# The delta branch's output norm in two halves, other places for its pieces, and other queues for some loads

## The reference, cut to what matters

```python
def merge(att, dn, z):
    gated = rms_norm(dn, dn_norm_g) * silu(z)        # per head of 64
    cat = concatenate([att, gated], axis=-1)         # 512 + 512 wide
    return cat @ w_out
dn_sum_c, dn_sum_l = bidir_delta(dn_c, dn_l, with_ctx_out)   # chunks of 64 tokens, both directions
out_l = merge(att_l, dn_sum_l, dz_l)                 # latents
out_c = merge(att_c, dn_sum_c, dz_c)                 # context tokens
```

## Time and profile before

| | us |
|---|---|
| median of 3 runs (1579.77 to 1584.63) | 1582.9 |
| the profiled execution | 1587.52 |
| its span | 1585.4 |
| PE busy in it | 1436.4 (91%) |
| DVE busy in it | 890.6 (56%) |
| ACT busy in it | 589.3 (37%) |
| POOL busy in it | 113.3 (7%) |
| mean TensorE clock, as a share of full speed | 0.951 |

### The profile page before, as it was taken

The page is one execution under the profiler, slowest core; times in us unless marked ns, Lnnn a source line. Parts: engine busy times, 40 slices in busy tenths (PEclk is TensorE's granted clock), DMA queues, the critical chain, the costliest instruction groups (busy, mean ns, idle before and its releaser), DMA issues. The chain is left out here.

```text
span 1585.4 us, 30140 instructions
## 1 busy us (share of the span) xinstructions
PE 1436.4 (91%) x13235; PEld 1180.1 (74%) x13235; DVE 890.6 (56%) x1279; ACT 589.3 (37%) x937; POOL 113.3 (7%) x113
## 2 busy tenths in 40 slices
PE   4798998899998698998999999899999998899998
PEld 2566676787887377766777888678888677799998
DVE  3548543544454547345446322769785764688854
ACT  3224535121212224233324211544463553455534
POOL 0000000233232000000000000000001430000000
PEclk7899989799999798999999999899999998899999
DMA  9221110244225121555554222223243003466652
GB/s 320 83 80 53 54 38 16 68 136 158 87 60 158 53 80 53 159 160 159 159 160 133 90 97 86 67 80 105 82 133 107 1 1 117 123 172 181 183 184 107
DMA packets 170764, 172.24 MB, mean 109 GB/s; under 512 B 15270, under 2 KB 135946, under 8 KB 170634
## 3 DMA queue, kind: packets, MB, share of 16 engines
q1 hardware_dynamic: 169328, 169.33, 35.1%
q10 hardware_dynamic: 1306, 0.99, 0.2%
HBM read 169.26 MB, written 1.05 MB: 107 GB/s over the span
## 5 line engine op out<-in xcount | busy, mean ns | idle before, releaser
L306 DVE TENSOR_TENSOR w_lo<-w_raw,w_hi 128x2048 fp32r<-128x2048 f32 (+1 forms) x99 | 225.3, 2276 | 289.6 <-ACT w_hi L296 289.4
L619 PE MATMUL bank<-h,w_hi 128*128 128x512 f32 (+2 forms) x1032 | 361.6, 350 | 26.6 <-issue 14.4
L622 PE MATMUL bank<-h,w_hi 128*128 128x512 f32 (+2 forms) x1032 | 352.0, 341 | 0.0
L623 PE MATMUL bank<-h,w_lo 128*128 128x512 f32 (+2 forms) x1032 | 351.8, 341 | 0.0
L296 ACT ACTIVATE w_hi<-w_raw 128x2048 fp32r<-128x2048 f32 (+1 forms) x99 | 187.9, 1898 | 292.4 <-PE bank L619 189.5
L619 PEld LDWEIGHTS bank<-h,w_hi 128*128 128x128 f32 (+1 forms) x1032 | 198.8, 193 | 65.9 <-issue 45.4
L622 PEld LDWEIGHTS bank<-h,w_hi 128*128 128x128 f32 (+1 forms) x1032 | 198.9, 193 | 23.3 <-issue 2.9
L623 PEld LDWEIGHTS bank<-h,w_lo 128*128 128x128 f32 (+1 forms) x1032 | 198.5, 192 | 22.2
L637 DVE SCALAR_TENSOR_TENSOR acc<-bank,params,acc 128x510 f32<-128x510 f32 (+3 forms) x272 | 172.1, 645 | 71.1 <-ACT acc L1372 46.0
L1372 ACT ACTIVATE acc<-bank,params 128x512 f32<-128x512 f32 (+1 forms) x88 | 47.7, 580 | 131.1 <-DVE ffn_g_lo L1389 49.8
L619 PE MATMUL bank<-h_hi,w_hi_hyb 128*128 128x512 f32 (+1 forms) x184 | 78.3, 425 | 12.7 <-DVE h_lo L594 4.9
(11 more groups left out here) (377 smaller groups left out, 2602.5 us busy)
## 6 DMA issues: line engine op xcount, KB each, us to landing
w_raw<-in_ffn_up SPq DMA_DIRECT2D x88, 512.0 KB, 5.3
w_raw<-in_mod_w SPq DMA_DIRECT2D x40, 1024.0 KB, 5.2
w_raw<-in_ffn_down SPq DMA_DIRECT2D x22, 1024.0 KB, 5.0
w_raw<-in_ssm_w_in SPq DMA_DIRECT2D x20, 1024.0 KB, 5.3
w_raw<-in_hyb_w_in SPq DMA_DIRECT2D x9, 1024.0 KB, 5.3
mod_early<-in_mod_w SPq DMA_DIRECT2D x8, 1024.0 KB, 11.0
w_raw<-in_ssm_w_out SPq DMA_DIRECT2D x8, 1024.0 KB, 4.8
w_raw<-in_hyb_w_in SPq DMA_DIRECT2D x8, 256.0 KB, 5.1
```

What stands on the lines that cost most here:

```text
L306: dve.tensor_tensor(lo, raw, hi.bitcast(F32), ALU.subtract).then_inc(k.lo_done.sem, 1)
L619: mm = pe.matmul(out, wh, xh, start=(start and n == 0), stop=False)
L622: pe.matmul(out, wh, xl, start=False, stop=False)
L623: mm = pe.matmul(out, wl, xh, start=False, stop=(stop and n == last))
```

## The change

The stage `stage_delta_out` is gone. Its work is done by a class `DeltaOut` that handles 256 tokens at a time, in pieces for each engine. The context tokens' pieces stand in the fourth pair and the tail of the solve. The latents' pieces stand in the first block of the product by the output matrix; for it, slot 0 takes both row blocks for one output tile after the other, with the sums after tile 1 and the spreads after tile 4. The split of the output matrix' first tile moves to the solve's tail. The last three modulation products move from the tail to the levels. In the start, the column groups 2 and 3 of `mod_w` are loaded by POOL's queue once the tokens have landed, the spread of the reciprocal root stands ahead of the third group's products, and the second tile's low part is made last on DVE. The solve's constants are loaded at the end of the attention block instead of at the start of the solve. Two more things move: the silu of z moves from the tail to the fourth pair, and the two weight buffers are numbered the other way round.

```diff
@@ stage_start
+            pool.wait_ge(k.s_in, 16 * (T // P))
+            for g in range(2, n_mod):
+                load_mod(pool, g)
...
-            issue_loads(k, sp, first + 2)
-            for g in range(2, n_mod):
-                load_mod(sp, g)
             issue_loads(k, sp, first + 4)
...
-            modulate(2)
             pe.wait_ge(recip_done.sem, recip_done.at(1))
...
+            modulate(2)
             modulate(3)
...
-            split_lo(k, dve, first + 1)
             mod_bias(k, dve, 0)
...
             low(KD - 1)
+            split_lo(k, dve, first + 1)
@@ stage_hyb_attention, SP
+            sp.wait_ge(mm_done.sem, mm_done.at(NC))
+            sp.dma_start(d.kc[:, :], a["k_dn"][:, 0:d.n_kc]).then_inc(s_k.sem, 16)
@@ RowGemm.pe
+            if self.out is not None and s == 2:
+                pe.wait_ge(self.out.l_done.sem, self.out.l_done.at(1))
+            if self.out is not None and s == 0:
+                for m in range(KD):
+                    if m == 6:
+                        pe.wait_ge(self.out.y_done.sem, self.out.y_done.at(2))
+                    split_matmuls(pe, self.bank(m)[:, 0:n], [pair(m, 0), pair(m, 1)], start=True, stop=False)
+                    if m == 1:
+                        self.out.pe_sums(pe)
+                    if m == 4:
+                        self.out.pe_spread(pe, 0)
+                        self.out.pe_spread(pe, 1)
@@ stage_delta_solve
-    for n, it in enumerate(sorted(list(range(13)) + [3, 6, 9]) + list(range(15, 20))):
+    for n, it in enumerate((0, 1, 2, 2, 3, 4, 5, 5, 6, 7, 8, 8, 9, 10, 11, 11, 14, 15, 16, 16, 17, 18, 18, 19)):
...
+                            if (lv, l) == (1, 0):
+                                o.pe_sums(pe)
+                            if (lv, l) == (2, 1):
+                                o.pe_spread(pe, 0)
+                            if (lv, l) == (3, 1):
+                                o.pe_spread(pe, 1)
             for n, (name, s) in enumerate(tail):
                 piece(name, s)
-                if n < 3:
-                    mod_products(k, pe, 29 + n)
-            mod_turn(k, pe, 2)
+                if n == 1:
+                    mod_turn(k, pe, 2)
@@ stage_delta_solve, ACT
+                        if lv == 0:
+                            act.activation(zT[:, :, :], zT[:, :, :], ACT.Silu).then_inc(zs_done.sem, 1)
+                            o.act_square(act)
+                        if lv == 1:
+                            o.act_root(act)
+                        if lv == 4:
+                            o.act_high(act)
...
                 if s == 6:
-                    act.activation(zT[:, :, :], zT[:, :, :], ACT.Silu)
+                    split_hi(k, act, first)
@@ stage_delta_solve, DVE
+                            if (lv, l) == (0, 0):
+                                dve.wait_ge(oc_done.sem, oc_done.at(4))
+                                o.dve_add(dve)
+                            if (lv, l) == (1, 1):
+                                o.dve_mean(dve)
+                            if (lv, l) == (2, 0):
+                                o.dve_recip(dve)
+                            if (lv, l) == (3, 0):
+                                o.dve_scale(dve, 0)
+                            if (lv, l) == (4, 0):
+                                o.dve_scale(dve, 1)
+                                dve.wait_ge(zs_done.sem, zs_done.at(1))
+                                o.dve_gate(dve)
             for name, s in tail:
                 piece(name, s)
+                if (name, s) == ("ks", 5):
+                    o.dve_low(dve)
+                if (name, s) == ("ds", 6):
+                    split_lo(k, dve, first)
@@ stage_layer0_tail, ACT and DVE
-            row0.act_splits(act, 1, 5)
+            out.act_square(act)
+            row0.act_splits(act, 1, 2)
+            out.act_root(act)
+            out.act_high(act)
+            row0.act_splits(act, 2, 5)
...
-            row0.dve_splits(dve, 1, 5)
+            out.dve_add(dve)
+            out.dve_mean(dve)
+            out.dve_recip(dve)
+            row0.dve_splits(dve, 1, 2)
+            out.dve_scale(dve, 0)
+            out.dve_scale(dve, 1)
+            out.dve_gate(dve)
+            out.dve_low(dve)
+            row0.dve_splits(dve, 2, 5)
```

158 lines of the change are left out of this document (81 added, 77 removed), and 4 rows, old and new, of the table TALLIES.

## The result

| | median us | runs | lowest to highest | profiled execution, span |
|---|---|---|---|---|
| before | 1583.96 | 15 | 1579.77 to 1589.46 | 1587.52, 1585.4 |
| changed | 1576.15 | 15 | 1570.45 to 1580.68 | 1573.66, 1571.9 |

The ratio is 0.9945 [0.9931, 0.9959]: 8.7 us faster. In seven more executions it was 0.9949 [0.9933, 0.9964]. The forecast was 17.1 us, and its range ended at 1574 us. The direction was right, half of the size is missing.

What follows compares the result with a forecast made beforehand. PE bounds the fourth pair, a dependent chain the tail, transfers the start. Terms -25.0 + 6.4 + 0.4 + 2.9 + 3.5 - 2.4 - 2.9 = -17.1 us took the median from 1582.9 to 1565.8, range 1556 to 1574.

Steps and rivals of the forecast that it cites:

- The stage, -25.0: Delta output stage, from the solve's end to the first product: goes entirely with one barrier, -25.0 us.
- the product, +3.5: Product by the output matrix: PE gains the latents' sums and spreads, 1.7 us each, the rest nearly hidden; +3.5 us.
- The start and the constants, -5.3 together: Program start -2.9 us, as a second queue fills transfer gaps; solve's constants loaded earlier, -2.4 us.
- their bound of 2.6: Solve's constants: the gain of 2.4 us was bounded between 0 and 2.6 us.
- The rival of POOL's late loads: Start: POOL's transfers begin only at 22 us, start gains 0, median 1568.7; chance 0.08, plus 0.02 for slower than before.
- PE and waits in the fourth pair: Solve's levels: added PE work of +6.4 us and waits of +0.4 us, the fourth pair taking 46 us instead of 40.8.
- +6.4 and +0.4 of the forecast: Levels: three products +3.0 and context sums and spreads +3.4 on PE; PE's waits for the square root's chain +0.4.
- The tail, +2.9: Solve's tail: gate starts it 1.45 us later, late weight split delays step 7; +2.9 us, bounds -0.8 and +4.
- half clock at 0.8 us for one piece: Tail, after PE idles 4 us more: one piece runs at half clock, adding 0.8 us.
- One product in pairs one to three, +1.0: Solve's levels: each modulation product moved there from the tail costs PE 1.0 us, uncovered; three cost +3.0.
- Handovers not hidden: Fourth pair: all 6.4 us of DVE's new work falls on the chain, +6.0 us, median 1571.8; chance 0.12.
- the signs named ahead of the run: First product at 48.4, `mod_bias` at 45, L1973 about 3 us late, no constants wait, slot 0 waits below 0.5, fourth pair 46.

Runs made afterwards that it cites:

- loads cut: Modulation loads 8 to 31 cut from 1 MB to 32 KB, products unchanged: ratio 0.9923, again 0.993, on the kernel before; 0.9864, again 0.9881, on the changed one.
- Start undone: Changed kernel with the old start: all loads on SyncE's queue, PE and DVE in their old order; 1577.37 us, ratio 0.9971.
- rearranged tail: On top of the moved split: second scaling, gate, context low part and the weights' low part in two halves put in DVE's gaps; 1566.8 us, ratio 0.9886.
- moved split: Changed kernel with the output matrix's first weight split moved: high part ahead of step 5's output copy, low part behind the last bias; 1570.66 us, 0.993.
- Undoing the table: Modulation products back at old levels, the last three in the tail: changed kernel 1570.67 us, 0.9916; with rearranged tail 1559.88, 0.9853; changed with loads cut 0.9849.

## Why the prediction was wrong

Mean times in us from the traces of kernels with whole loads that share the stretch ("level n" is ACT's copy of `X_mat` there). Kernels with old parts stand on the left, with new ones on the right, in brackets the number of profiles:

| stretch | old | new | difference | forecast |
|---|---|---|---|---|
| start to first instruction of the solve | 277.9 (6) | 275.9 (14) | -2.0 | -2.9 |
| from there to level 0 | 20.8 (6) | 17.4 (14) | -3.4 | -2.4 |
| level 0 to level 15 | 154.0 (7) | 161.7 (7) | +7.7 | +1.0 |
| level 15 to 19 | 34.0 (4) | 39.7 (6) | +5.7 | +5.8 |
| level 19 to the row product: tail and stage | 56.6 (4) | 37.1 (4) | -19.5 | -22.1 |
| row product to slot 2 | 23.5 (4) | 26.4 (4) | +2.9 | +3.5 |
| sum | | | -8.6 | -17.1 |

The first two rows include profiles with loads cut, since the cut loads come after them. The forecast's +2.9 for the tail and -25.0 for the stage are taken together, because part of the +2.9 was a barrier of 0.5 in place of the 1.5 us that lay before between the last output copy and the end of the block. Measured up to the tail's last matmul and from there on, the two parts are +6.4 and -25.9. The sum of the differences meets the timed 8.1 to 8.7.

*The stage, -25.0, and the product, +3.5 (measured +2.9): right.* No wait for the root's chain or the gate appears in slot 0, and slot 0 begins at full clock in the first profile, 0.47 us for the first matmul.

*The start and the constants, -5.3 together: right in sum*, -5.4 in the traces and 4.1 ± 2.6 when added alone. But that is two errors that cancel. The start was put too high: mixing the queues filled nothing (all landed at 42.37, forecast 40.3), and the order of the ready tiles brought the 2 us. The constants brought 3.4, more than their bound of 2.6. DVE's first operation came 2.6 earlier (279.25, 281.82 before). The rest is clock: the stretch from there to level 0 ran at 0.78 (281 to 294 us) instead of 0.62 (284 to 298). The rival of POOL's late loads did not come: the trace has POOL issuing from 9.56 to 12.7, with DVE busy for 1.44 of these 3.15 us. The rule cited from the Trainium skill, "SBUF — State Buffer", section "SBUF: two separate sides", would have given a start without gain. Start undone, the kernel was 3.5 ± 3.2 us slower. But DVE did little beside POOL's issuing, two copies out of PE's banks (L570) and the start of a third copy, so this trace shows no conflict and is no hard test of the rule.

*PE and waits in the fourth pair: right*, 5.7 against 5.8 (the +6.4 and +0.4 of the forecast less the one product that lies in pair three). The sums took 1.90, each half of the spreads 1.08, the products 1.0 each.

*The tail, +2.9: wrong by 2.6 us, taken with the stage.* The step that failed is what a wait of PE costs beyond itself. The late L1973 was foreseen rightly: by the forecast it starts 3.8 us after it is ready (513.0 with step 6 0.8 earlier), and it came 3.7 late (at step 6 it starts 1.22 behind its PE group, so 517.2 at step 7, and it started at 520.92). But I priced half clock at 0.8 us for one piece and only behind step 7's wait. It came in two places. Behind step 7's wait all four profiles with this tail are slow to the end: from the first product of step 7 to its last they take 6.8 us on average, against 4.6 in three of the four before (5.9 in the fourth, whose clock fell behind a wait of 1.39) and in the kernel with the rearranged tail. In step 5, behind 1.97 us of idling for the gate, 15.1 us pass on average from level 19's copy to step 6's first matmul, 14.1 before. I had counted 0.8 less than before. The kernel with the moved split has the same step 5, with the same idling, and there it ran at full clock and took 12.9. So the count was right at full clock, and half clock cost some 2.2 us in each of the two places, 4.4 in place of 0.8. The other pieces, each 0.3 or 0.4 better than counted, bring the error from 3.6 down to 2.6. Moved split and rearranged tail together brought 9.6 ± 3.9 us.

*One product in pairs one to three, +1.0: wrong by 6.7 us.* This is the largest error. I had costed the new table by the number of products, and had put at nothing where the loads that it triggers fall. PE idles 4.5 us more in stops behind loads (9.6 against 5.1 on average), the product is 1.0, and the other 2 are half clock that differs from run to run. The two groups do not touch: 151.7 to 157.0 us with the old table, 160.2 to 165.9 with the new one. Undoing the table gained 4.9 ± 4.5 us with whole loads, 5.2 ± 5.0 with the tail rearranged and 5.1 ± 3.7 with cut loads: each is just clear of its uncertainty, and all three agree. So that the table is to blame is shown; that it is by the loads is shown in the traces of pairs one to three, where the 7.7 us shrink to 1.5 with the loads cut. What share of the timed 5 us the stops have stays open. So does why the new table's stops are longer. It is not that more fetches meet a load: of the 32 packets of instructions in these pairs, 12 or 13 come behind one with either table.

Of the rivals none came true as written. "Handovers not hidden" had the right size (+6) at the wrong place: the fourth pair took what was forecast, and pairs one to three took 6.7 more. Nor did the signs named ahead of the run point there: L1973 came late as told, the fourth pair took 45.5 us, the first product of the start came at 49.28, earlier than the 51 that would have told against the forecast. None of them looked at pairs one to three.

## What to carry to other kernels

Work that goes into another engine's gaps has to be cut to the gap's length and be ready in time: 1.22 us in a gap of 1.25 cost nothing. 2.29 us of work whose input came 2.80 late made PE wait 4.41 us instead of 0.72, and half clock behind it took 2 more. When a table of small products is shifted, the transfers that their buffers release shift too. Count those as part of the change, and look in the profile after for stops without a reason ("issue") in the middle of matmul runs. And one profile of each kernel is not enough to say where 2 us went: here it told of a gain given back that never was.

## What the runs showed of the hardware

PE's program comes by the same DMA engines as the data, in packets of 16 KB of a queue of its own (q8), and it comes late where a load of 1 MB is moving. PE went on 1.19 to 1.63 us after the packet's end in all 153 stops. With modulation loads of 1 MB PE stopped 6 to 13 us in all between 290 and 530 us, for up to 2.6 us at once. With loads of 32 KB the stops were 0 to 0.7 us in all, and the kernel before was 11 to 12 us faster. The Trainium skill, "Runtime: NRT & Kernel Launch", section "Instruction fetch mechanics", calls crossing a block of instructions mostly hidden. These traces do not agree where a load is in flight: half of the packets behind a load (150 of 301) were followed by a stop.

Idling of 2 us could bring half clock, but did not do so each time. After the 1.97 to 1.98 us ahead of step 5, two of five profiles ran their next 32 matmuls in 1.89 and 1.98 us, in two the clock fell one or two groups later, and in the fifth (split moved) all of step 5 ran at full clock. After the 4.41 us ahead of step 7 it was half clock in all four. Behind waits of only 1.39 us in the tail it was mostly full clock, but in some profiles half. After a stop of 2.61 us the clock over the next 6.8 us was 0.54:

```profile
505.00:510.60 5.60, 4.68 (x144) 4.30 (x139) 3.72 (x6) 2.46 (x3) 1.04 (x1) 1.00 0.87 187
510.60:513.20 2.60, 0.03 (x1) 0.00 (x0) 0.17 (x1) 0.00 (x0) 0.00 (x0) 0.90 0.03 6
513.20:520.00 6.80, 5.99 (x78) 5.66 (x77) 3.38 (x6) 0.66 (x2) 0.00 (x0) 0.54 0.01 2
```

Two queues with large packets moved 387 GB/s together (22 to 30 us), where one queue alone had 381 before (31 to 42.6 us). All had landed at 42.4 us with two queues and at 42.6 with one. Whether small packets beside large ones would move sooner these runs do not show, because they hardly met.
